# A decoder layer on one core: the dense products read their moving tile and write PSUM in 16-byte chunks, 80 bytes apart, in five passes

## The reference: what is computed

```
h = RMSNorm(x);  z = h @ w_in          # 2048 -> queries | latent | rope key | pooling channels | 2 gates
A = latent attention (16 heads, causal; the 8 sequences read 1024 cached tokens each)
B = causal pooling over windows 2/4/8/16, a linear map for each group
merged = sigmoid(gA) * (A @ w_attn_out) + sigmoid(gB) * (B @ w_pool_out)
x = x + merged @ w_o
z = RMSNorm(x) @ w_up                  # 2048 -> 2 x 5632
x = x + (silu(causal_conv3(z_a)) * z_v) @ w_down
y = RMSNorm(x)
```

## Time and profile before

| | us |
|---|---|
| median of 3 runs | 1944.38 (1943.84 to 1944.42) |
| the profiled execution: its own time | 1944.88 |
| its span, first to last instruction | 1943.1 |
| PE busy | 1927.0 (99%), 13,412 products |
| DVE busy | 1091.2 (56%) |
| ACT busy | 760.4 (39%) |
| POOL busy | 96.4 (5%) |
| DMA | 318.18 MB, 164 GB/s in the mean |

### The profile page before, as it was taken

The page is one execution under the profiler, slowest core; times in us unless marked ns, Lnnn a source line. Parts: engine busy times, 40 slices in busy tenths (PEclk is TensorE's granted clock), DMA queues, the critical chain, the costliest instruction groups (busy, mean ns, idle before and its releaser), DMA issues.

```text
span 1943.1 us, 34161 instructions
## 1 busy us (share of the span) xinstructions
PE 1927.0 (99%) x13412; PEld 1909.0 (98%) x13412; DVE 1091.2 (56%) x1506; ACT 760.4 (39%) x846; POOL 96.4 (5%) x252
## 2 busy tenths in 40 slices
PE   9999999999999999999999999999999999999997
PEld 8999999999999999999999999999999999999997
DVE  6865344434345774455556565656656556565656
ACT  5456542332257653333343333332323333333334
POOL 0002000000000350000000000000000000000000
PEclk9999999999999999999999999999999999999999
DMA  7444444444443697454444444434344444443443
GB/s 254 152 152 178 151 151 151 151 151 151 151 173 136 214 312 257 166 205 151 151 159 152 141 163 141 162 140 162 139 163 151 151 151 151 139 163 138 165 145 112
DMA packets 60042, 318.18 MB, mean 164 GB/s; under 512 B 6674, under 2 KB 6994, under 8 KB 27346
## 3 DMA queue, kind: packets, MB, share of 16 engines
q1 hardware_dynamic: 59330, 313.15, 45.0%
q10 hardware_dynamic: 656, 4.27, 0.5%
HBM read 313.08 MB, written 4.32 MB: 163 GB/s over the span
## 4 chain that ended last, share of the span: by engine, by line
PE 93%; DVE 3%; ACT 1%; DMA 1%; issue 1%; SPq 0%; POOL 0%; DVEq 0%; ACTq 0%; POOLq 0%
PE ps L1647 93%; ACT w_hi L583 1%; DVE w_lo L1026 0%; DVE keys_lo L1026 0%; DMA xT<-in_x 0%; DMA w_raw<-in_cache_t 0%; PE ps L1963 0%; DMA c_raw<-in_cache 0%; DVE y_gain L1026 0%; POOL k_rope_all L549 0%; ACT sm L835 0%; DVE sm L1373 0%; SPq L424 0%; SPq L408 0%; PE ps L1913 0%
## 5 line engine op out<-in xcount | busy, mean ns | idle before, releaser
L1026 DVE TENSOR_TENSOR w_lo<-w_raw,w_hi 128x2048 fp32r<-128x2048 f32 (+1 forms) x251 | 571.1, 2276 | 436.9 <-ACT w_hi L583 436.9
L1647 PE MATMUL ps<-h_lo,w_hi 128*128 128x320 f32 x2512 | 768.7, 309 | 0.2 <-DVE h_lo L1118 0.2
L1647 PE MATMUL ps<-h_hi,w_hi 128*128 128x320 f32 x2512 | 756.5, 304 | 0.9 <-ACT w_hi L583 0.7
L583 ACT ACTIVATE w_hi<-w_raw 128x2048 fp32r<-128x2048 f32 (+2 forms) x253 | 479.3, 1895 | 597.4 <-PE ps L1647 585.1
L1647 PE MATMUL ps<-h_hi,w_lo 128*128 128x320 f32 x2496 | 686.5, 307 | 1.4 <-DVE w_lo L1026 1.4
L1647 PEld LDWEIGHTS ps<-h_hi,w_hi 128*128 128x128 f32 x2512 | 471.6, 188 | 2.2 <-ACT w_hi L583 1.2
L1647 PEld LDWEIGHTS ps<-h_lo,w_hi 128*128 128x128 f32 x2512 | 470.1, 187 | 1.0 <-DVE h_lo L1118 0.7
L1647 PEld LDWEIGHTS ps<-h_hi,w_lo 128*128 128x128 f32 x2496 | 448.6, 188 | 1.9 <-DVE w_lo L1026 1.9
L1647 PE MATMUL ps<-hid_lo,w_hi 128*128 128x320 f32 x704 | 217.5, 309 | 0.0
L1647 PE MATMUL ps<-hid_hi,w_hi 128*128 128x320 f32 x722 | 216.3, 303 | 0.0
L1647 PE MATMUL ps<-hid_hi,w_lo 128*128 128x320 f32 x704 | 215.4, 306 | 0.0
(11 more groups left out here) (249 smaller groups left out, 1953.3 us busy)
## 6 DMA issues: line engine op xcount, KB each, us to landing
w_raw<-in_slabs SPq DMA_DIRECT2D x252, 1024.0 KB, 4.8
w_raw<-in_cache_t SPq DMA_DIRECT2D x64, 288.0 KB, 4.2
c_raw<-in_cache SPq DMA_DIRECT2D x56, 256.0 KB, 4.5
w_whole<-in_slabs SPq DMA_DIRECT2D x4, 1024.0 KB, 7.5
x_again<-in_x ACTq DMA_DIRECT2D x1, 2560.0 KB, 9.3
c_last<-in_cache SPq DMA_DIRECT2D x8, 256.0 KB, 4.1
xT<-in_x SPq DMA_DIRECT2D x3, 640.0 KB, 9.5
w_raw<-in_slabs SPq DMA_DIRECT2D x3, 512.0 KB, 8.3
```

The source lines that it names most:

```text
L583: return nc.scalar.activation(out, in_, ACT.Copy)
L1026: return nc.vector.tensor_tensor(out, a, b, op)
L1647: return nc.tensor.matmul(out, a, b, start=start, stop=stop, **kw)
```

## The change: what it does

A new helper, `passes`, rearranges a tile of 320 columns. It takes the columns as 16 groups (b) of five chunks (l) of four values (c), and walks them with l outermost: first chunk 0 of all 16 groups, then chunk 1 of all, up to chunk 4. Four float32 values are 16 bytes, five chunks are 80 bytes. So one pass reads 16 chunks of 16 bytes at steps of 80 bytes, and five passes cover the 1280 bytes. The output in PSUM is rearranged in the same manner, so each column goes where it went before. The stationary operand, the number of products, their order, and every wait and semaphore stay as they are.

```
+            def passes(tile):
+                return tile.rearrange("p (b l c) -> p l b c", l=5, c=4)
+
             def dense(s, hi, lo):
-                return [(ps[:, s, 0:T], [(wb(k), hi[:, k, :], lo[:, k, :]) for k in range(KD)])]
+                return [(passes(ps[:, s, 0:T]), [(wb(k), passes(hi[:, k, :]), passes(lo[:, k, :]))
+                                                 for k in range(KD)])]
...
-                return [(ps[:, b, 0:T], [(wb(k), h_hi[:, k, :], h_lo[:, k, :]) for k in range(KD)])]
+                return [(passes(ps[:, b, 0:T]), [(wb(k), passes(h_hi[:, k, :]), passes(h_lo[:, k, :]))
+                                                 for k in range(KD)])]
...
-            group("pool_out", lambda s: [(ps[:, s + 2 * j, 0:T], [(wb(8 * j + k), op_hi[:, k, :], op_lo[:, k, :])
-                                                                  for k in range(PT_)]) for j in range(2)])
+            group("pool_out", lambda s: [(passes(ps[:, s + 2 * j, 0:T]),
+                                          [(wb(8 * j + k), passes(op_hi[:, k, :]), passes(op_lo[:, k, :]))
+                                           for k in range(PT_)]) for j in range(2)])
...
-                         [(ps[:, 2 * (f % 2) + s, 0:T], [(wb(k), h2_hi[:, k, :], h2_lo[:, k, :]) for k in range(KD)])],
+                         [(passes(ps[:, 2 * (f % 2) + s, 0:T]),
+                           [(wb(k), passes(h2_hi[:, k, :]), passes(h2_lo[:, k, :])) for k in range(KD)])],
...
-                        out = ps[:, banks[n], 0:T]
+                        out, hi, lo = (passes(t) for t in (ps[:, banks[n], 0:T], hid_hi[:, k, :], hid_lo[:, k, :]))
                         w = 4 * n + k
-                        mm(out, blk(w_hi[s], w), hid_hi[:, k, :], k == 0, False)
-                        mm(out, blk(w_hi[s], w), hid_lo[:, k, :], False, False)
-                        last = mm(out, blk(w_lo[s], w), hid_hi[:, k, :], False, k == FPC - 1)
+                        mm(out, blk(w_hi[s], w), hi, k == 0, False)
+                        mm(out, blk(w_hi[s], w), lo, False, False)
+                        last = mm(out, blk(w_lo[s], w), hi, False, k == FPC - 1)
```

## The result

The changed kernel takes 2191.69 us (median of 4 runs, 2191.10 to 2191.96), the kernel before beside it 1944.40. The ratio is 1.127 (95% interval 1.125 to 1.129): 247 us slower. The forecast was 1892, and the range, to 2005, doesn't hold it.

The account below looks back on a forecast made before the run. The prediction took PE's pace of successive dense products, 144.6 ns each, as the bound. At 140 ns, 4.6 x 11,328 = 52 us come off 1944.4, giving 1892 us, with a range of 1848 to 2005.

Parts of the forecast that it names:

- PE's pace is the bound: Feed-forward stretch: only the pace of successive dense products, 144.6 ns each, sets the time; PE is busy all 800 us.
- 305 us of other work: Whole kernel: 11,328 dense products take 1638 us of 1943.1; the other 305 us stay as they are.
- the surplus of 11.3 ns: Every dense product: 144.6 ns against 133.3 for streaming 320 columns at 2.4 GHz; 8% is not streaming.
- those reads meet the loads of the next weights: Dense products: surplus comes from moving-tile and next-weight reads meeting; the faster case, 1892 us, chance 0.44.
- a stride of five chunks meets them less: Moving-tile read: the new order has fewer meetings of reads, making the kernel faster, 1892 us; chance 0.44.
- The value that I take is 140 ns: Every dense product: 4.6 ns less than 144.6, so 52 us off; a pace hi x w_hi already reaches.
- slower by much: the price is per chunk: SBUF or PSUM access: 80 chunks at one clock each, 33 ns per product, 2322 us; rival's chance 0.18.
- the two slow cases: Dense products: slower by a little, 1980 or 2072 us, chance 0.17; slower by much, 2322 or 3365 us, chance 0.18.
- evenly for all three kinds: Profile after: distances of all three dense kinds grow alike if the price is per chunk or in the PSUM write.
- no change: Dense products: whole 16-byte chunks are read whatever their order, or order doesn't touch the surplus; 1944 us, chance 0.21.
- half pace: Dense products: the stream falls to the plain product's 270 ns, 3365 us; within slower by much, chance 0.18.
- The lower end, 136.3 ns: Every dense product: 133.3 + 3 ns, avoiding all surplus but the plain product's; 94 us less, 1850 us.

Follow-up runs that it names:

- same_chunk: Kernel before, but dense products read the first 16 bytes of their moving row 80 times, PSUM written in one row: 1856.25 us.
- sweep_loops: Against the kernel before, slabs read small parts of the moving row repeatedly: one value, one line, two lines in turn, or loops of 64 to 640 bytes; 1914.51 us.
- step320: Changed kernel with 16-byte chunks at steps of 320 bytes, twenty passes of four chunks, read and write: 1936.75 us, ratio to before 0.9961.
- weights_one_value: Kernel before, but each dense and 256-column key product loads one column 128 times as its stationary block: 1964.72 us.
- the sweep: Slabs given different read orders, PSUM written in one row: single passes 1 to 16 lines apart, 2024.65 us; for step320's expectation, orders covering the row, 1977.29 us.
- read_only: Changed kernel with only the read of the moving tile in five passes, PSUM written in one row: 2190.91 us, ratio to before 1.127.
- plain_types: Kernel before with plain float32 dense products in three groups, alternating plain row and five passes; a fourth group alternates (16,4) and (8,4): 3005.82 us.

## Why the prediction was wrong

- That PE's pace is the bound, that each nanosecond per dense product is 11.3 us and that nothing hides or adds to it: right. 22.0 ns gave 247 us.
- That 305 us of other work stay: right but for the 256-column key products, 118 ns in place of 113.5, under 1 us in all. Their operands and addresses are the same, so this is a distance that moved with its surroundings alone.
- That the surplus of 11.3 ns comes from reading the moving tile: right, and shown. It sinks to 2.5 when a product reads only one line or two in turn (same_chunk, sweep_loops), and an order of reading can lower it (step320, 143.4 ns in the up-projection).
- That those reads meet the loads of the next weights: wrong as the source of the surplus, which stays, 2 ns larger, when the load reads a single line (weights_one_value). The loads do act on the plain row, as the same run shows kind by kind, but not in the direction that the forecast needed. That "a stride of five chunks meets them less" had no row at all; in the sweep five lines apart is one of the dearest distances, 166.7 ns against 144.4 for the plain row.
- The step that failed is that sentence on the stride, and with it the value taken: "The value that I take is 140 ns". I took the best distance that a product of the kernel shows as what a new order would bring, with no row for the order itself, and admitted as much ("I cannot say from a row why a stride of five should be better and not worse"). Between one end at -94 us and another at +378 and beyond, that value had no row behind it. The measured term is +22.0 ns, not -4.6: 166.6 ns per product and not 140, all of it in the read (read_only, 166.5).
- The rival "slower by much: the price is per chunk" comes near in size, by accident. Five clocks per chunk is what the trace shows, but put on a bare 320 clocks, not on the 347 of before: 22 ns where I wrote 33, 2192 and not 2322. And its mechanism fell: 80 chunks at steps of 32 or 64 bytes cost 144 to 147 ns. The hole between 2072 and 2322 in my cases is where the result lies, and the range ended at 2005 because I gave the two slow cases only 0.35 between them.
- The sign that I gave for a price per chunk or in PSUM, "evenly for all three kinds", did appear (337 ns three times), with the read as its cause. Evenness tells neither side: weights_one_value is even too (309 ns three times), and there as here the read is the cause.
- That nothing but the 16-byte line counts, by which no change had a chance of 0.21: wrong by 22 ns.
- That plain float32 products follow each other after 0.27 us: misread. The rows count records, and a plain product is two (plain_types; at its start the kernel issues eight such products, and the trace has 16 records of them). A product takes 0.54 us, so the "half pace" of the rivals would have been about a quarter of the pace. The lower end, 136.3 ns, was taken from the 3 ns that a record has over 266.7; that it comes near the 135.8 of a row that stays in one line is luck.

Not settled: what makes 6 lines cost 200 ns, 5 and 13 lines 166.7, 16 lines 177.8, and 3, 7 and 9 nearly nothing; and why the same step of 320 bytes, in the same tile, costs 143.0 ns in one slab and 145.7 in another. I found no number of banks that gives this row of prices. That five lines apart costs 22 ns in the read is shown; why it does is open.

## What to carry to other kernels

Where float32r products run back to back, the array needs a 16-byte line every four clocks, and the order of the moving read decides how near it comes to that pace. Give the tile the plain row unless a measured step is better. One kernel that gives each slab another order finds the candidates; since a distance depends also on what surrounds the product, only a kernel that uses the step throughout gives its worth (1929 us were expected of step320 from the sweep, 1936.75 came). The output in PSUM may be permuted in chunks of four columns at steps of 80 bytes; other orders of writing weren't tried by themselves. A surplus in a trace that moves with its surroundings shows that an access pattern matters; it doesn't say in which direction a new one will go, and without a row for the new pattern both ends belong in the range.

## What the runs showed of the hardware that was not expected

- Read of the moving tile, float32r, 320 columns at 2.4 GHz: 135.8 ns for one line again and again, 144.4 for the plain row, 142.5 to 200.0 for single passes at steps of 1 to 16 lines.
- Two lines in turn are as cheap as one (135.8 to 136.7 ns) at nine distances from 1 to 64 lines, a loop of four lines is dearer than the plain row (153.1).
- Writing PSUM in 16-byte chunks at steps of 80 bytes costs nothing: ratio 0.9998 (0.9988 to 1.0007).
- Replacing 32 lines of a weight load by one made the plain rows 2 ns slower each, 20 us in all.
- In plain float32, where a record of 320 columns takes 269.2 ns, none of the four orders tried costs anything.
- The same products at the same addresses have more than one pace: 143.0 or 145.7 ns in the up-projection of step320, 113.5 or 118 for the untouched key products.
